# Borders of the mix, cross and last stages placed anew; in the last stage VectorE forms the weights' product and ScalarE scales the weight units

## The reference

```
for l in range(2):
    x = x + 0.5 * swiglu(rmsnorm(x), w_ffn1)
    h = rmsnorm(x)                               # mix
    y_conv = zb * causal_conv(zc * zv)
    y_att  = forgetting_attention(q, k, v, log_f)  # 8 heads of 64
    x = x + concat(rmsnorm(y_conv), rmsnorm(y_att)) @ w_mix_out
    x = x + memory_cross_attention(rmsnorm(x), rmsnorm(mem))  # 4 heads of 256
    x = x + 0.5 * swiglu(rmsnorm(x), w_ffn2)
x = rmsnorm(x)
x = diff_layer(x)
k, v = split(rmsnorm(x, kv_norm) @ w_kv)         # last stage
q, g = split(rmsnorm(x, b_norm) @ w_in)          # 16 heads of 64
z = q @ k.T / 8                                   # per head, key < query
a = exp(log_sigmoid(z) + sum over later keys of log_sigmoid(-z))
x = x + ((a @ v) * silu(g)) @ w_out
```

## Time and profile before

| | us |
|---|---|
| median of 3 runs | 2913.24 (2910.73 to 2915.46) |
| profiled execution | 2911.05 |
| its span in the trace | 2909.2 |
| PE busy in the span | 2843.3 |
| VectorE busy | 1676.3 |
| ScalarE busy | 1092.2 |
| GpSimd busy | 397.3 |

### The profile page before, as it was taken

One profiled execution on the slowest core, in us unless ns is written; L12 is line 12 of the kernel. 1 busy time (PEld: TensorE's weight loads), 2 busy tenths in 40 slices (PEclk: granted clock), 3 DMA queues, 4 the chain that ended last, 5 costly groups with the idle time before them and its releaser, 6 DMA issues.

```text
span 2909.2 us, 34967 instructions
## 1 busy us (share of the span) xinstructions
PE 2843.3 (98%) x14241; PEld 2363.5 (81%) x14241; DVE 1676.3 (58%) x2400; ACT 1092.2 (38%) x1699; POOL 397.3 (14%) x263
## 2 busy tenths in 40 slices
PE   8999999999999999999999999999999899899988
PEld 7888887888888888888887889888888787678777
DVE  5554357675464533555247776555533677768884
ACT  4322244554332322323234454422222444444442
POOL 2000111110100001000011220100001322154430
PEclk9999999999999999999999999999999999999999
DMA  4332332243233233332323233233323222131211
GB/s 141 101 95 94 95 88 73 66 127 106 87 94 97 88 101 98 101 95 87 105 71 92 68 108 118 80 109 95 101 91 98 70 64 69 47 88 59 72 59 51
DMA packets 302240, 258.08 MB, mean 89 GB/s; under 512 B 11367, under 2 KB 299904, under 8 KB 302080
## 3 DMA queue, kind: packets, MB, share of 16 engines
q1 hardware_dynamic: 300704, 254.76, 28.7%
q10 hardware_dynamic: 1024, 1.05, 0.2%
q0 software_dynamic: 352, 0.03, 0.0%
HBM read 252.66 MB, written 2.10 MB: 88 GB/s over the span
## 4 chain that ended last, share of the span: by engine, by line
PE 82%; DVE 10%; ACT 3%; issue 3%; POOL 2%; DMA 1%; ACTq 0%; SPq 0%; POOLq 0%; DVEq 0%
PE PS L1525 26%; PE PS L1527 25%; PE PS L1526 25%; DVE WL L2255 3%; PE PS L1531 2%; PE PS L1770 1%; DVE AF L2701 1%; DVE SM L2619 1%; ACT AF L2129 0%; PE PS L1623 0%; PE PS L1812 0%; PE PS L1811 0%; DVE AR L2711 0%; ACT WH L1872 0%; POOL SM L2869 0%
## 5 line engine op out<-in xcount | busy, mean ns | idle before, releaser
L2255 DVE TENSOR_TENSOR WL<-RAW,WH 128x1024 fp32r<-128x1024 f32 x480 | 617.9, 1293 | 572.9 <-ACT WH L1872 572.6
L1525 PE MATMUL PS<-XH,WL 128*128 128x512 f32 x2256 | 904.4, 401 | 2.9 <-DVE XL L2265 2.9
L1527 PE MATMUL PS<-XH,WH 128*128 128x512 f32 x2256 | 883.3, 392 | 0.0
L1526 PE MATMUL PS<-XL,WH 128*128 128x512 f32 x2256 | 882.1, 391 | 0.0
L1872 ACT ACTIVATE WH<-RAW 128x1024 fp32r<-128x1024 f32 x448 | 465.4, 1044 | 1005.9 <-PE PS L1527 994.6
L1525 PEld LDWEIGHTS PS<-XH,WL 128*128 128x128 f32 x2256 | 425.8, 189 | 101.5 <-issue 12.7
L1527 PEld LDWEIGHTS PS<-XH,WH 128*128 128x128 f32 x2256 | 425.2, 188 | 91.5
L1526 PEld LDWEIGHTS PS<-XL,WH 128*128 128x128 f32 x2256 | 426.3, 189 | 81.1
L1525 PE MATMUL PS<-AR,WL 128*128 128x512 f32 (+1 forms) x1216 | 465.3, 383 | 7.3 <-DVE SC L2599 3.5
L1527 PE MATMUL PS<-AR,WH 128*128 128x512 f32 (+1 forms) x1216 | 460.7, 379 | 0.0
L1526 PE MATMUL PS<-AR,WH 128*128 128x512 f32 (+1 forms) x1216 | 460.6, 379 | 0.0
(11 more groups left out here) (259 smaller groups left out, 3000.0 us busy)
## 6 DMA issues: line engine op xcount, KB each, us to landing
RAW<-in_w_ffn_gu_dram SPq DMA_DIRECT2D x176, 512.0 KB, 3.5
RAW<-in_w_ffn_down_dram SPq DMA_DIRECT2D x80, 512.0 KB, 3.4
RAW<-in_w_mix_in_dram SPq DMA_DIRECT2D x48, 512.0 KB, 4.0
RAW<-in_w_xkv_dram SPq DMA_DIRECT2D x32, 512.0 KB, 3.4
RAW<-in_a_w_in_dram SPq DMA_DIRECT2D x32, 512.0 KB, 4.2
RAW<-in_w_mix_out_dram SPq DMA_DIRECT2D x16, 512.0 KB, 3.4
RAW<-in_w_xq_dram SPq DMA_DIRECT2D x16, 512.0 KB, 4.1
RAW<-in_w_xo_dram SPq DMA_DIRECT2D x16, 512.0 KB, 3.4
```

What stands on the lines that cost most here:

```text
L1525: pe.matmul(o, ll, rh, start=start, stop=False, skip_group_check=skip)
L1526: pe.matmul(o, lh, rl, start=False, stop=False, skip_group_check=skip)
L1527: return pe.matmul(o, lh, rh, start=False, stop=stop, skip_group_check=skip)
L2255: dve.tensor_tensor(l, raw_slot(n), F(h), ALU.subtract).then_inc(sg["wl"].up(n))
```

## The change

- Mix: the pause between bt and ms of one step goes for tiles under 16, so that both are placed as a pair, at rates from 4.3 / 64 to 6.3 / 80; the last rounds go at 4.4 / 54. The second half of the first values goes to bank 7.
- Cross: `norm_a` after 12 steps, `norm_b` after 5; the first two output chunks use banks in the order of their last use.
- Last stage, border: three products of q1 stand ahead of norm_a, three of k1 ahead of norm_b; the gates of t - 1 are all computed in t.
- Last stage, tiles: bt and bs placed as a pair. The product bmul moves from GpSimd to VectorE. ScalarE scales the weights (8 operations of 128 columns, or 4 of 256), GpSimd no more. q is not multiplied by RB; the sigmoids have the row norm as their scale (RCOL, and its negative NB4, which VectorE makes once). bps puts both halves in the first bank, so that gy is one operation of 128 rows; the second bank is freed by bps.

```diff
@@ mix
-                    yield
+                    if n >= 16:
+                        yield
-        self.drain(self.flow(self.values(s, 0)))
+        self.drain(self.flow(self.values(s, 0, 7)))
-        side = self.stream(att(0, 4), 6.5 / 64)
+        side = self.stream(att(0, 4), 4.3 / 64)
-            side = self.stream(att(4 * m, 4 * m + 4), 10.5 / 80)
+            side = self.stream(att(4 * m, 4 * m + 4), 6.3 / 80)
-        side = self.stream(att(16, 19), 4.5 / 44)
+        side = self.stream(att(16, 19), 4.4 / 54)
@@ cross
-            for _ in range(2):
+            for _ in range(5):
                 yield next(g)
             self.norm_b(s)
-        for _ in range(10):
+        for _ in range(12):
             next(g)
         self.norm_a(s)
+        a, b, c, d = self.turn
         self.own_banks(4, 5)
-        self.out_proj(s, self.stream(att(3), 8.2 / 48), flow=True)
+        self.out_proj(s, self.stream(att(3), 8.2 / 48), ((a, b), (c, d)), flow=True)
@@ last stage
-                self.give(b, "gy", (t,))
+                self.give(b, "bps", (s, t, 1))
-                    yield
+                    if n >= 32:
+                        yield
-                    self.later(5, "bmul", (s, n), "gprob")
+                    self.later(5, "bmul", (s, n), "bprob")
+        g = self.tile(q1, b1)
+        for _ in range(3):
+            next(g)
         self.norm_a(s)
-        g = self.tile(q1, b1)
-        for _ in range(6):
+        self.drain(g)
+        kb = self.take()
+        g = self.tile(((s, "k1"), 0), kb)
+        for _ in range(3):
             next(g)
         self.norm_b(s)
-        side = self.stream(att(0, 4), 6 / 64)
+        side = self.stream(att(0, 4), 4.3 / 48)
-            if t < 7:
-                main.append(gated(t - 1))
-            side = self.stream(att(4 * t - 4, 4 * t), 10.5 / (32 + (32 if t % 2 else 0) + (16 if t < 7 else 0)))
+            main.append(gated(t - 1))
+            side = self.stream(att(4 * t - 4, 4 * t), 6.3 / (48 + (32 if t % 2 else 0)))
-            yield from self.chain(gated(6), gated(7))
+            yield from gated(7)
-        side = self.stream(att(28, 33), 13 / 56)
+        side = self.stream(att(28, 33), 8.2 / 40)
@@ ScalarE
+            def scale(n):
+                g0 = units[n][2]
+                w = raw_slot(n)
+                on.wait_ge(*raw_ready(n))
+                for k in range(w.shape[1]):
+                    t = act.activation(w[:, k, :], w[:, k, :], ACT.Copy, scale=GA[:, g0 + k:g0 + k + 1])
+                t.then_inc(sg["wg"].up(n))
-                act.activation(OM[n % 2][:, :, T - N:T], z, ACT.Sigmoid, scale=-1.0).then_inc(sg["exps"].up(s, n))
-                act.activation(BE[n % 3][:, :, T - N:T], z, ACT.Sigmoid).then_inc(sg["sbe"].up(s, n))
+                act.activation(OM[n % 2][:, :, T - N:T], z, ACT.Sigmoid, scale=NB4[:, i:i + 1]).then_inc(sg["exps"].up(s, n))
+                act.activation(BE[n % 3][:, :, T - N:T], z, ACT.Sigmoid, scale=RCOL[:, i:i + 1]).then_inc(sg["sbe"].up(s, n))
@@ VectorE
-                y = PS[P.bank_of[s, t, hh]][r, :]
-                dve.tensor_tensor(y, y, F(YL[r, t, :]), ALU.add).then_inc(sg["pvs"].up(s, t, hh))
+                dve.tensor_tensor(PS[P.bank_of[s, t, 0]][r, :], PS[P.bank_of[s, t, hh]][r, :], F(YL[r, t, :]),
+                                  ALU.add).then_inc(sg["pvs"].up(s, t, hh))
             def bqe(s, w, t):
+                if s == LAST and w == "q":
+                    return
+            def bmul(s, n):
...
+                dve.tensor_tensor(b, b, OM[n % 2][:, :, T - N + 1:T + 1], ALU.mult).then_inc(sg["bprob"].up(s, n))
-                for hh in range(2):
...
-                    y = dve.tensor_tensor(ET[r, t % 2, :], ET[r, t % 2, :], PS[P.bank_of[LAST, t, hh]][r, :], ALU.mult)
+                e = ET[:, t % 2, :]
+                dve.tensor_tensor(e, e, PS[P.bank_of[LAST, t, 0]], ALU.mult).then_inc(sg["gy"].up(t))
@@ GpSimd
-            def scale(n):
-                pool.tensor_tensor(w, w, GA[:, g0:g0 + nk].unsqueeze(2).to_broadcast([128, nk, nc_]), ALU.mult).then_inc(sg["wg"].up(n))
-            def bmul(s, n):
...
-                pool.tensor_tensor(b, b, OM[n % 2][:, :, T - N + 1:T + 1], ALU.mult).then_inc(sg["gprob"].up(s, n))
```

More of the change, by code:

```diff
@@ L758, in xattn, with out_proj @@
             self.finish(side)
+        a, b, c, d = self.turn
         self.own_banks(4, 5)
-        self.out_proj(s, self.stream(att(3), 8.2 / 48), flow=True)
-    def out_proj(self, s, side, flow=False):
+        self.out_proj(s, self.stream(att(3), 8.2 / 48), ((a, b), (c, d)), flow=True)
+    def out_proj(self, s, side, pairs, flow=False):
         def out(p, bb):
-            return self.chunk((s, f"o{p}"), (bb, bb + 1), "o", [("x", (s + 1, 2 * p + c)) for c in range(2)])
+            return self.chunk((s, f"o{p}"), bb, "o", [("x", (s + 1, 2 * p + c)) for c in range(2)])
         def close(p):
             self.resid(s, (2 * p, 2 * p + 1), ((ch[p], 0), (ch[p], 1)))
-        ch = {p: out(p, 2 * p) for p in range(4)}
+        ch = {p: out(p, bb) for p, bb in enumerate((*pairs, (4, 5), (6, 7)))}
         g = self.mm_two(ch[0], ch[1])
@@ L1015, in due @@
     def due(self, *step):
+        if step[0] == "gy":
+            for hh in range(2):
+                self.due("bps", (LAST, *step[1], hh))
         if any(x[1][:2] == step for x in self.soon):
@@ L1037, in heads_in, with values @@
     def heads_in(self, s, w, t):
-        self.add("bqe", (s, w, t), "et", "eh")
+        self.add("bqe", (s, w, t), *(() if s == LAST and w == "q" else ("et",)), "eh")
         self.later(6, "bql", (s, w, t), "el")
-    def values(self, s, c):
+    def values(self, s, c, spare=None):
         ch = ((s, f"v{c}"), 0)
         for n in range(2):
-            b = self.take()
+            b = self.take() if spare is None or n == 0 else spare
             yield from self.rows_tile(ch, n, b, (lambda: self.add("evh", (ch, 1), "vh")) if n else lambda: None)
@@ L1129, in stick @@
         self.add("barrier", (s,))
-        self.add("mq", (s,), "mask", "zero", "tri")
+        self.add("mq", (s,), "mask", "zero", "tri", "minus")
         for w, t in (("q", 0), ("k", 0), ("q", 1)):
             self.heads_in(s, w, t)
-        side = self.stream(att(0, 4), 6 / 64)
-        self.weave(self.flow(self.chain(qk("k", 1), self.values(s, 0), gated(0))), side)
+        self.drain(self.flow(g))
+        self.give(kb, "bql", (s, "k", 1))
+        self.heads_in(s, "k", 1)
+        side = self.stream(att(0, 4), 4.3 / 48)
+        self.weave(self.flow(self.chain(self.values(s, 0), gated(0))), side)
         for t in range(2, 8):
@@ L1790, in bt @@
                 p = row_buf(s, n)
-                on.wait_ge(*sg["gprob"].at(s, n))
+                on.wait_ge(*sg["bprob" if nm(s) == "sb" else "gprob"].at(s, n))
                 bank_free(6)
@@ L1815, in bpv @@
                 w.then_inc(sg["pv"].up(s, t, hh))
-                free[b] = [{"mix": ("yl", (s, t, hh)), "diff": ("dov", ("o", t)), "sb": ("gy", (t,))}[nm(s)]]
+                free[b] = [{"mix": ("yl", (s, t, hh)), "diff": ("dov", ("o", t)), "sb": ("pvs", (s, t, 1)) if hh else ("gy", (t,))}[nm(s)]]
                 free[b] = [sg[g].at(*key) for g, key in free[b]]
@@ L2156, in bqe @@
                 h, _, f = slot_qk(w, t)
-                on.wait_ge(*sg["et"].at(s, w, t))
+                if s == LAST and w == "q":
+                    on.wait_ge(*sg["mm"].at(((s, f"{w}{t}"), 0), 0, KT - 1))
+                else:
+                    on.wait_ge(*sg["et"].at(s, w, t))
                 if t > 1:
@@ L2349, in mq @@
                     dve.memset(F(GONE[:, 0:384]), 0.0).then_inc(sg["zero"].up(s))
+                    on.wait_ge(*sg["rcol"].at(s))
+                    dve.tensor_scalar(NB4, RCOL, -1.0, None, ALU.mult).then_inc(sg["minus"].up(s))
                     on.wait_ge(*sg["mask"].at(s))
@@ L2751, in _ @@
                   "ny_a": ny_a, "evc": evc, "eva": eva, "mem_a": mem_a, "mem_b": mem_b, "dn": dn, "dkb": dkb, "dsin": dsin,
-                  "dad": dad, "dlo": dlo, "ds": ds, "dc": dc, "dtl": dtl, "don": don, "dob": dob, "dom": dom, "dol": dol, "dga": dga, "dgb": dgb, "bqe": bqe, "bql": bql, "bsc": bsc, "btl": btl, "ga": ga, "gb": gb, "gy": gy, "gl": gl, "sv": sv}
+                  "dad": dad, "dlo": dlo, "ds": ds, "dc": dc, "dtl": dtl, "don": don, "dob": dob, "dom": dom, "dol": dol, "dga": dga, "dgb": dgb, "bqe": bqe, "bql": bql, "bsc": bsc, "bmul": bmul, "btl": btl, "ga": ga, "gb": gb, "gy": gy, "gl": gl, "sv": sv}
             for kind, key in order:
```

34 lines of the change are left out of this document (15 added, 19 removed).

## The result

The changed kernel takes 2916.62 us in the median of 20 runs (2913.95 to 2919.41), the kernel before 2912.84 us on the same chip (2908.67 to 2915.89). The ratio is 1.0014, with a 95% interval from 1.0008 to 1.0020: slower by 0.14%, against a forecast of 0.66% faster and a range that ended at 2914. The profiled execution has a span of 2914.4 us.

What follows compares the result with a forecast made beforehand. PE, busy 98% of the span, was taken as the bound, with only its gaps to win. Terms -12 - 5 + 1 - 4.6 - 1.5 + 3 = -19.1 us gave 2894 us as median; range for 8 in 10, 2879 to 2914.

Steps and rivals of the forecast that it cites:

- VectorE's sum: Last stage: stretching and halved operations go, 32 weight products come; VectorE's busy time falls by a net 15 us.
- ScalarE's sum: Last stage: scaling adds 68 us and sigmoids 6; ScalarE goes from 138.6 to about 205 us of 322.
- What hides the scaling is its idle time: Last stage: ScalarE's idle time covers the scaling; uncovered, a unit's 2.3 us would stand before ph, btl and the next transpose.
- the low part's stretch goes, most waits fall below the point of stalling: Last stage: with 1.9 us of stretch out of VectorE's queue, most waits of 1 to 2.9 us stop stalling PE.
- The clock: Last stage: with waits over 2 us gone, 5 of 7.0 us lost at lower clock return; bounds 0 and -7.
- The border: Start of last stage: squares' 1.3 us wait goes, ScalarE's raw-unit waits add 3; +1 us, bounds -2 and +4.
- Cross: Cross stages: norm_a's 0.8 and xpl's 1.5 us waits go per layer; -4.6 us, bounds -4.6 and -3.
- Mix: Mix stages: bql's 0.8 us wait goes, btl waits move; -1.5 us, bounds -4 and +6.
- Pairing: Mix and last stage: some 57 transposes placed with scores cost PE 0.05 us each; +3 us, bounds 0 and +8.6.
- steady part: Last stage's tiles: of 17.1 us of PE waits for btl and gb a third stays; -12 us, bounds -17 and 0.
- waits only move: Last stage: added products and paired order keep VectorE's queue late, no clock gain; -4.6 us, 2909; chance 0.19.
- ScalarE's queue: Last stage: scaling waits for raw units ahead of ph or sigmoids; +10 us, 2923; chance 0.13.

Runs made afterwards that it cites:

- scale_tiny: Changed kernel with mix's last rounds at the old rate, each weight unit's scaling cut to one operation of two columns: 2890.63 us, 0.9930 of the kernel before.
- scale_pool: Changed kernel with GpSimd scaling the weight units again, VectorE keeping the weights' product: 2920.89 us, 1.0032 of the kernel before.
- no_last: Kernel before with only the change's mix and cross parts, mix's last rounds at the old rate, last stage as before: 2905.58 us, 0.9977 of the kernel before.
- bmul_pool: Changed kernel with GpSimd forming the weights' product again, ScalarE keeping the scaling: 2915.37 us, 1.0014 of the kernel before.

## Why the prediction was wrong, point by point

**VectorE's sum** was right: -15 us forecast, 242.1 to 224.6 measured for 2583 to 2914, -17.5. The product takes 1226 ns for 1024 columns (1220 forecast).

**ScalarE's sum** was right too, 205 us forecast and 205.6 measured. The 32 scalings take 58.6 + 13.6 = 72.2 us (192 operations of 391 ns, 32 of 507), where I had 68. The Trainium skill ("ScalarE: Activation LUTs", What ACT_TABLE_LOAD costs) would give 72 (estimate): the trace agrees with it.

**"What hides the scaling is its idle time"** is the step that failed first. The cover was costed as a sum, and it had to hold place by place: scale_tiny gives some 12 us for the work. A strip's 2.45 us, or 4.05 with a value unit, falls ahead of ph, xh or a split, each of which has a chain behind it. The prediction named that and left a third of 17.1 us; transposes and value products wait 11.8 + 4.6 = 16.4 us for btl. The 17.1 had left out a value product's wait for the same step,

```profile
PE PS L1811 <- DVE AR L2711: 1.1, 1, 1.1
```

so that it is 18.2 to 16.4: -12 came out as -1.8. Not all of the failure is ScalarE's. Up to the last scaling the waits go from 11.1 to 9.0 us, and to 3.6 without the scaling's work (scale_tiny). Behind it they go from 7.0 to 7.4, with or without that work: there the product stands in VectorE's queue ahead of btl, and gl waits for ScalarE. The prediction had named the product's place in that queue, but had it only in its bound of 0. The point "the low part's stretch goes, most waits fall below the point of stalling" was right as to the cause (scale_pool has 19.4 us where scaling stretches VectorE again) and wrong in that the gain is kept.

**The clock** was to give 5 us back with the long waits; as those only changed their places, it gave nothing (6.9 us missing for 7.0).

**The border** was sized at +1 us, bounds -2 and +4: PE waits 6.7 us where 1.3 went, +5.4. The chain was the one named, ScalarE's wait for k1 and v0 ahead of xh; but the waits were 7.32 and 4.57 us, not 1.5, the mean on GpSimd. That mean hid how uneven they were: 40.5 of the 47.1 us are seven waits in the trace of before, one of them 10.2 us long:

```profile
POOL RAW L2783 <- DMA RAW<-in_b_w_in_dram: 40.5, 7, 10.2
```

That VectorE's norm step stands behind the low part of the same unit wasn't in the working.

**Cross** was to give -4.6 us. norm_a no longer waits (0.8 each); the 1.5 us for xpl turned into 1.3 for the low part of the last q (L2404), whose bank comes next. -2.0 by the waits, -2.3 by the stages. "Nothing is added" was the error: a bank that is taken later in turn has a last reader of its own.

**Mix** was -1.5 us, bounds -4 and +6. The waits of its two stages go from 3.3 + 3.1 to 5.9 + 4.3, +3.8 (+4.1 by the stages, with 1.7 at the lower clock behind the second one's waits), and the rate at the end alone is worth 8.2 between the medians (8.0 by the stages, 6.3 by PE's waits). The rate was read in the diff and not followed to what it delays: the loads on SP's queue. Without it mix and cross together give -5.5 (no_last), for the forecast -4.6 - 1.5 = -6.1.

**Pairing** at +3 us was a price for PE's switches, and there is none to be seen: less waits and clock, the last stage takes 291.1 us paired and 291.5 before, a mix stage 238.1 to 238.9 paired and 239.0 to 239.2 before. What the order changes is the waits: unpaired steps cost 7.3 us more with the scaling on ScalarE.

**The sum** by waits: last stage 21.1 to 24.0 us, +2.9; mix +3.8; cross -2.0; +4.7, for a measured +3.8 between the medians and +5.2 between the spans. Between this and the forecast of -19.1 lie 23.8 us, and no single term has them: steady part 10, mix 5, clock 5, border 4, cross 3, less 3 for pairing. The rivals named both mechanisms; "waits only move" (0.19) is the nearest, with ScalarE's queue as the place (0.13), and their chances were too low. The range left out the case that both a new border wait and a longer mix come on top of a steady part without gain. Two slips in the working change nothing of this: 87 us of scaling without overlap is 89 by its own terms, and no steady gain with the other terms kept gives 2911, not 2909.

## What to carry to other kernels

Work that is moved to an engine with idle time is hidden only where that time lies: write down, for each moved instruction, what it is queued ahead of and how long that may wait, above all where the moved step itself waits for a transfer. The mean of a wait on an engine with nothing urgent behind it says little on the places where it is long. And a placing rate is followed to the loads that it delays, not only to the engine that it paces.

## What the runs showed of the hardware that was not expected

A wait's length doesn't alone set the granted clock. In the changed kernel PE waits 3.03 us up to 2647.7, and the stretch around it stays at full clock, as does the one behind it to 2700, while after the 2.85 us wait that ends at 2838.1 it falls (two stretches of ten us):

```profile
2620.00:2650.00 30.00, 26.97 (x175) 22.32 (x174) 22.15 (x38) 26.00 (x55) 0.00 (x0) 1.00 0.23 71
```
```profile
2830.00:2840.00 10.00, 7.15 (x38) 5.44 (x38) 8.74 (x14) 4.95 (x8) 0.00 (x0) 0.88 0.43 142
2840.00:2850.00 10.00, 9.72 (x46) 7.34 (x45) 7.09 (x10) 6.14 (x9) 0.00 (x0) 0.78 0.03 10
```

What parts the two was not tried. And VectorE's slowing beside GpSimd is a hold, not a share. In bmul_pool (GpSimd's product, VectorE's low part):

```profile
2709.84 2.40 POOL L2910 TENSOR_TENSOR SC<-SC,AF 128x1024 f32<-128x1024 f32 x1 [14.46 <-DVE SC L2735]
...
2710.21 3.12 DVE L2280 TENSOR_TENSOR WL<-RAW,WH 128x1024 fp32r<-128x1024 f32 x1
```

A low part of 1.22 us took 3.12 beside a product of 2.40 that had begun 0.37 us earlier, and 2.40 - 0.37 + 1.22 = 3.25. So it goes throughout the last stage of that run: 23 low parts begin while GpSimd works, with 0.26 to 2.30 us of its operation left, and each takes what is left and 1.08 to 1.09 us; the 18 that begin while it is idle take 1.21 to 1.23. The Trainium skill ("SBUF — State Buffer", Who interferes with whom) has it that the port pair the two engines share is an exclusive lock, and that a VectorE instruction with two SBUF inputs contends with a GpSimd instruction that reads SBUF; the trace agrees, as the low part runs as if it began 0.13 us before GpSimd's end.
